# Three norm roots leave the inputs of products and go into their results; two products end tile by tile

## The reference

```python
def _rmsnorm(x, g):
    xf = x.astype(jnp.float32)
    y = xf * lax.rsqrt(jnp.mean(xf * xf, axis=-1, keepdims=True) + EPS)
    return (y * g.astype(jnp.float32)).astype(x.dtype)

        hn = _rmsnorm(x, norm_mix[l])
        z = hn @ w_in[l]
        ...
        x = x + _memory_cross_attention(_rmsnorm(x, norm_cross[l]), _rmsnorm(mem, norm_mem[l]),
                                        w_q_mem[l], w_kv_mem[l], w_o_mem[l])
        x = x + _peer(_rmsnorm(x, norm_ffn[l]), w_query[l], sub_keys[l], expert_u[l], expert_v[l])
```

## Time and profile before

| | us |
|---|---|
| median of 3 runs (lowest, highest) | 2040.69 (2038.19, 2043.49) |
| profiled execution, its own time | 2043.17 |
| its span, first to last instruction | 2041.3 |
| TensorE busy in it | 1978.3 |

### The profile page before, as it was taken

The page is one execution under the profiler, slowest core; times in us unless marked ns, Lnnn a source line. Parts: engine busy times, 40 slices in busy tenths (PEclk is TensorE's granted clock), DMA queues, the critical chain, the costliest instruction groups (busy, mean ns, idle before and its releaser), DMA issues.

```text
span 2041.3 us, 34876 instructions
## 1 busy us (share of the span) xinstructions
PE 1978.3 (97%) x14212; PEld 1831.8 (90%) x14212; DVE 1408.3 (69%) x2543; ACT 1140.7 (56%) x1919; POOL 303.1 (15%) x328
## 2 busy tenths in 40 slices
PE   8999999999999989998999989999999999999997
PEld 5798998999888889998988989999999998888886
DVE  6777765888777667547746458898996765555554
ACT  5865533556666455435654454456677754444444
POOL 0010010000000000000000000028867940000000
PEclk9999999999999999998999999999999999999999
DMA  9465787346444347665433444554444445555553
GB/s 355 159 213 186 245 282 233 115 153 220 153 147 145 114 118 228 189 185 181 156 114 133 134 154 161 184 179 151 156 142 158 145 148 189 188 186 186 188 189 118
DMA packets 97743, 356.25 MB, mean 175 GB/s; under 512 B 11104, under 2 KB 11232, under 8 KB 97200
## 3 DMA queue, kind: packets, MB, share of 16 engines
q1 hardware_dynamic: 84240, 305.04, 44.8%
q0 software_dynamic: 12624, 48.08, 7.3%
q10 hardware_dynamic: 720, 0.91, 0.1%
HBM read 352.94 MB, written 1.05 MB: 173 GB/s over the span
## 4 chain that ended last, share of the span: by engine, by line
PE 90%; DVE 5%; ACT 3%; issue 1%; DMA 1%; ACTq 0%; DVEq 0%
PE psum L576 23%; PE psum L577 23%; PE psum L578 23%; PE psum L569 18%; PE psum L583 2%; DVE wl L1993 1%; ACT wh L1368 1%; ACT work L1356 0%; DMA araw<-in_ada_w 0%; DMA con<-in_con 0%; DVE xc L1973 0%; DVE cross_sq L1973 0%; ACT na L1356 0%; DVE head_squares L1973 0%; ACT C L1356 0%
## 5 line engine op out<-in xcount | busy, mean ns | idle before, releaser
L1993 DVE TENSOR_TENSOR wl<-raw,wh 128x1024 fp32r<-128x1024 f32 (+1 forms) x566 | 687.7, 1218 | 436.7 <-ACT wh L1368 436.1
L1368 ACT ACTIVATE wh<-raw 128x1024 fp32r<-128x1024 f32 (+1 forms) x566 | 594.0, 1050 | 448.8 <-PE psum L578 410.9
L576 PE MATMUL psum<-peer_hh,wh 128*128 128x256 f32 x1152 | 330.7, 287 | 3.6 <-DVE peer_hl L1965 3.6
L577 PE MATMUL psum<-peer_hl,wh 128*128 128x256 f32 x1152 | 326.2, 283 | 0.0
L578 PE MATMUL psum<-peer_hh,wl 128*128 128x256 f32 x1152 | 326.1, 283 | 0.0
L576 PEld LDWEIGHTS psum<-peer_hh,wh 128*128 128x128 f32 x1152 | 219.5, 191 | 3.9 <-issue 3.9
L578 PEld LDWEIGHTS psum<-peer_hh,wl 128*128 128x128 f32 x1152 | 217.5, 189 | 0.0
L577 PEld LDWEIGHTS psum<-peer_hl,wh 128*128 128x128 f32 x1152 | 217.5, 189 | 0.0
L576 PE MATMUL psum<-wh,csh 128*128 128x512 f32 x512 | 202.9, 396 | 0.0
L578 PE MATMUL psum<-wh,csl 128*128 128x512 f32 x512 | 202.7, 396 | 0.0
L577 PE MATMUL psum<-wl,csh 128*128 128x512 f32 x512 | 202.7, 396 | 0.0
(11 more groups left out here) (456 smaller groups left out, 4675.8 us busy)
## 6 DMA issues: line engine op xcount, KB each, us to landing
raw<-in_mlp_w SPq DMA_DIRECT2D x128, 512.0 KB, 4.2
raw<-in_eu SPq DMA_DIRECT2D x128, 512.0 KB, 3.5
raw<-in_ev SPq DMA_DIRECT2D x128, 512.0 KB, 3.4
araw<-in_ada_w POOLq DMA_DIRECT2D x76, 512.0 KB, 4.8
raw<-in_dil_qk SPq DMA_DIRECT2D x48, 512.0 KB, 4.0
raw<-in_dil_v SPq DMA_DIRECT2D x24, 512.0 KB, 3.5
raw<-in_w_in SPq DMA_DIRECT2D x16, 512.0 KB, 3.6
raw<-in_w_query SPq DMA_DIRECT2D x16, 512.0 KB, 3.5
```

What stands on the lines that cost most here:

```text
L576: e.matmul(o, l[0], r[0], start=start, stop=False, skip_group_check=loose)
L577: e.matmul(o, l[0], r[1], start=False, stop=False, skip_group_check=loose)
L1368: e.activation(b.wh[v % NSPLIT][:, 0:cols], b.raw[v % NRAW][:, 0:cols], ACT.Copy).then_inc(S.hi, 1)
L1993: e.tensor_tensor(b.wl[v % NSPLIT][:, 0:cols], b.raw[v % NRAW][:, 0:cols], b.wh[v % NSPLIT][:, 0:cols].bitcast(F32), ALU.subtract).then_in ...
```

## The change

The second product of both MLPs gets another layout of its weights (`stationary`, regrouped on the host): four units hold all 32 input tiles of one output tile, so the output tiles end one after another, every four units, each in a bank of its own. Squares and sums are made tile by tile (`tile_square`, `tile_sum`); the sum of tile k is issued two units into the next tile. In the second MLP the tile is also multiplied by the next norm's gain and split at once (`tile_high`, `tile_low`), without the root.

For n4, n5 and n6 the root no longer stands in the product's input. It is made beside the first units of the next product (`root_x`, `rsqrt`) and multiplies results: in the mixer x_lru and gate by VectorE (`scaled`), q and k by GpSimd, v by ScalarE through a column per token; at n5 as a column in the softmax's scale; at n6 as a column in the experts' scores. `root_columns` turns the root's row into columns by two matmuls with one output column each. The experts' first product keeps an input with the root, made by VectorE, ScalarE and GpSimd beside query units 2 to 5. The last two units of w_o are done together, output pair by output pair (`rows_end`). `opening` is no longer used at these three borders. GpSimd scales mem, fills the bias masks and starts mem's load when the last MLP unit is done. The mixer's side work is placed anew. n2 keeps `norm_x`, with its sums made per tile.

```diff
-    beside = {3: ("conv", 0), 4: ("conv", 1), 5: ("conv", 2), 6: ("conv", 3), 8: ("gates", 0), 9: ("lam", 0),
-              10: ("decay", 0), 12: ("scan", 0)}
-    steps = {20: 0, 21: 1, 22: 2, 23: 3, 24: 4, 25: 5, 26: 6, 27: 7, 28: 8, 29: 9}
+    beside = {3: ("conv", 0), 4: ("conv", 1), 6: ("conv", 2), 8: ("conv", 3), 10: ("gates", 0), 11: ("lam", 0),
+              12: ("decay", 0), 14: ("scan", 0)}
+    steps = {19: 0, 21: 1, 22: 2, 23: 3, 24: 4, 25: 5, 26: 6, 27: 7, 28: 8, 29: 9}
...
-        if 1 <= i < 8:
+        if i in (1, 2, 3, 7, 9, 15, 16):
...
 def cross_order():
-    out = [("unit", "w_mem_v", 4), ("total", None, None)] + [("unit", "w_mem_v", i) for i in (5, 6, 7)]
+    out = [("unit", "w_mem_v", 4), ("tiles", None, 0), ("total", None, None), ("unit", "w_mem_v", 5),
+           ("tiles", None, 4), ("unit", "w_mem_v", 6), ("root", None, None), ("unit", "w_mem_v", 7)]
     for i in range(8):
         out.append(("unit", "w_q_mem_2", i))
+        if i == 0:
+            out.append(("columns", None, None))
         if i in (2, 4, 6):
             out.append(("step", None, i // 2 - 1))
...
     for c in range(16):
         out.append(("query", c, None))
+        if c == 0:
+            out += [("root", None, None)]
+        if c == 2:
+            out.append(("columns", None, None))
+        if c in (2, 3, 4, 5):
+            out += [("tile", 2 * c - 4, None), ("tile", 2 * c - 3, None)]
+        if c == 6:
+            out.append(("tile", 8, None))
...
+    def tile_sum(tag, k, ring):
+
+        if k == 0:
+            take(tag, "total")
+        ps = b.psum[:, at["bank", tag, "total"], :]
+        pe.wait_ge(S.act, at[tag, "square", k])
+        mm(ps[:, 0:256], ones, ring[:, (k % 4) * 256:(k % 4) * 256 + 256], k == 0, k == 7, mark=(tag, "squares", k),
+           loose=True)
+        if k == 7:
+            give(tag, "total", sem=S.act, key=(tag, "ms"))
+
+    def root_columns(tag, rs):
+
+        ps = take(tag, "roots")
+        pe.wait_ge(S.dve, at[tag, "root"])
+        for t in range(2):
+            mm(ps[:, t:t + 1], rs[:, t * 128:t * 128 + 128], ident[:, 0:1], True, True,
+               mark=(tag, "roots") if t else None)
+        give(tag, "roots", sem=S.dve, key=(tag, "root columns"))
...
+    def rows_end(tag, name, k, x, ring):
+
+        j = [weights(name, k), weights(name, k + 1)]
+        for c in range(8):
+            o = b.psum[:, at["bank", tag, c // 2], (c % 2) * 256:(c % 2) * 256 + 256]
+            for y in range(2):
+                w, done = wsp(j[y], c * 128, 128), y == 1 and c % 2 == 1
+                mm(o, w[0], x[y][0], False, False, loose=True)
+                mm(o, w[0], x[y][1], False, False, loose=True)
+                if c == 7:
+                    e.matmul(o, w[1], x[y][0], start=False, stop=done, skip_group_check=True).then_inc(S.unit, 1)
+                else:
+                    mm(o, w[1], x[y][0], False, done, loose=True, mark=(tag, "done", c // 2) if done else None)
+            if c in (5, 7):
+                square_sums(tag, c // 2 - 2, ring)
+        for c2 in range(4):
+            give(tag, c2, sem=S.dve, key=(tag, "out", c2))
 
...
         project((tag, 1), "mlp_w1", 4096, m.hh, lambda k: (S.dve, (norm, "lo", k)), S.act, first=32 * layer)
-        acc = [take(tag, 2, i) for i in range(4)]
-        for s in range(32):
-            j = weights("mlp_w2", 32 * layer + s)
-            pe.wait_ge(S.dve, at[(tag, 1), "h1", s // 2])
-            for c in range(8):
-                o, w, h = acc[c // 2][:, (c % 2) * 256:(c % 2) * 256 + 256], wsp(j, c * 128, 128), sp(m.h1, s)
-                if s == 31 and c in (1, 3, 5):
-                    mm(o, w[0], h[0], False, False, loose=True)
-                    mm(o, w[0], h[1], False, False, loose=True)
-                    mm(o, w[1], h[0], False, True, loose=True, mark=((tag, 2), "done", c // 2))
-                else:
-                    mm3(o, w, h, s == 0 and c % 2 == 0, s == 31 and c == 7, unit=c == 7, loose=True)
-        for c2 in range(4):
-            give(tag, 2, c2, sem=S.dve, key=((tag, 2), "out", c2))
-            square_sums((tag, 2), c2, m.rbf)
+        for c in range(8):
+            o = take(tag, 2, c)[:, 0:256]
+            for q in range(4):
+                j = weights("mlp_w2", 32 * layer + 4 * c + q)
+                for k in range(8):
+                    pe.wait_ge(S.dve, at[(tag, 1), "h1", 4 * q + k // 2])
+                    mm3(o, wsp(j, k * 128, 128), sp(m.h1, 8 * q + k), q == 0 and k == 0, q == 3 and k == 7,
+                        unit=k == 7)
+                if c and q == 1:
+                    tile_sum((tag, 2), c - 1, m.rbf)
+            give(tag, 2, c, sem=S.dve, key=((tag, 2), "out", c))
+        if layer == 0:
+            tile_sum((tag, 2), 7, m.rbf)
...
+    def tile_high(tag, ready, k, gain, dst):
+
+        ac.wait_ge(S.dve, at[ready])
+        act(dst[0][:, k * 256:k * 256 + 256], b.xs3[:, k, :], ACT.Copy, scale=gain, mark=(tag, "hi", k))
+
+    def root_x(tag, sums, tmp, last=3):
+        ac.wait_ge(S.pe, at[sums, "squares", last])
         act(tmp[:, 512:768], bank(sums, "total")[:, 0:256], ACT.Abs_reciprocal_sqrt, scale=1.0 / 1024, bias=eps,
             mark=(tag, "rs0"))
         act(tmp[:, 256:512], bank(sums, "total")[:, 0:256], ACT.Identity, scale=1.0 / 1024, bias=eps,
             mark=(sums, "ms"))
...
         for s in range(32):
             unit("mlp_w2", 32 * layer + s)
-        for c2 in range(4):
-            square((tag, 2), c2, m.rbf, ((tag, 2), "out", c2))
+            if s and s % 4 == 0:
+                after(s // 4 - 1)
+        after(7)
...
+        norm_x("n2", ("mlp0", 2), shift, m.hh, m.work[:, 0:2048], m.vtf[:, 0:768], last=7)
...
+                if (name, i) == ("w_in_2", 0):
+                    root_x("n4", ("mlp1", 2), m.tmp, 7)
...
         for kind, name, i in CROSS_ORDER:
-            if kind == "total":
-                norm_x("n5", "out2", None, m.hh, m.sq, m.tmp, UNIT_OF["w_mem_v", 5])
+            if kind == "tiles":
+                for k in range(i, i + 4):
+                    tile_high("n5", ("out2", "out", k // 2), k, vc(b, "cross", k), x.hh)
+            elif kind == "root":
+                root_x("n5", "out2", m.tmp)
+            elif kind in ("total", "columns"):
...
+            if c2 == 3:
+                unit("w_o_mem_2", 7)
+                ahead(UNIT_OF["w_query_2", 1] - AHEAD)
+            for k in (2 * c2, 2 * c2 + 1):
+                tile_high("n6 gain", ("mo", "out", c2), k, vc(b, "ffn", k), x.hh)
             square("mo", c2, m.ring, ("mo", "out", c2))
 
     def peer():
         m = b.peer
         phase("peer")
...
+    def tile_low(tag, k, gain, dst):
+
+        z = slice(k * 256, k * 256 + 256)
+        ve.wait_ge(S.act, at[tag, "hi", k])
+        stt(dst[1][:, z], b.xT[:, z], gain, dst[0][:, z].bitcast(F32), ALU.mult, ALU.subtract, mark=(tag, "lo", k))
...
+                if bias is None:
+                    tt(st[:, 1, i, :], st[:, 0, i, :], scale, ALU.mult, mark=(tag, "negmax", i))
+                else:
+                    ts(st[:, 1, i, :], st[:, 0, i, :], -scale, None, ALU.mult, mark=(tag, "negmax", i))
...
+        def after(c):
+
+            ve.wait_ge(S.unit, UNIT_OF["mlp_w2", 32 * layer + 4 * c + 3] + 1)
+            src = bank(tag, 2, c)[:, 0:256]
+            g, xs, mark = b.mod[:, 48 * layer + 40 + c:48 * layer + 41 + c], b.xs3[:, c, :], ((tag, 2), "out", c)
             if layer:
                 t = m.sq[:, c * 256:c * 256 + 256]
                 stt(t, src, g, xs, ALU.mult, ALU.add)
                 own()
                 cp(xs.rearrange("p (l s r) -> p l s r", l=16, s=4), t.rearrange("p (r s l) -> p l s r", r=4, s=4),
                    mark=mark)
+                own()
             else:
                 stt(xs, src, g, xs, ALU.mult, ALU.add, mark=mark)
+
+        mod_until(48 * layer + 40)
+        own()
+        for s in range(32):
+            c = s // 4 - 1
+            if c >= 0 and s % 4 == 0:
+                after(c)
+            unit("mlp_w2", 32 * layer + s)
+            if layer and c >= 0 and s % 4 == 0:
+                tile_low("n4", c, vc(b, "norm_mix_2", c), b.mix.hh)
+            tick(every)
+        after(7)
+        if layer:
+            tile_low("n4", 7, vc(b, "norm_mix_2", 7), b.mix.hh)
+        mod_until(last)
...
+
+        def scaled(c2, u):
+
+            c = 2 * (c2 % 2)
+            ve.wait_ge(S.unit, u + 1)
+            tt(m.ge[:, c:c + 2, :] if c2 > 1 else m.xp[:, c:c + 2, 3:259],
+               bank("in2", c2).rearrange("p (c t) -> p c t", c=2), rs.unsqueeze(1).broadcast_to([128, 2, 256]), ALU.mult,
+               mark=("in2", "out", c2))
...
+                if name == "w_in_2" and i % 2 and i < 8:
+                    scaled(i // 2, UNIT_OF[name, i])
...
-            if kind == "total":
-                norm_x("n5", lambda k: vc(b, "cross", k), None, m.hh, m.sq, m.tmp, UNIT_OF["w_mem_v", 5])
+            if kind == "tiles":
```

(51 more changed lines are left out.)

205 lines of the change are left out of this document (107 added, 98 removed).

## The result

| us | before | after |
|---|---|---|
| median (lowest, highest), 4 runs each | 2040.5 (2038.2, 2043.5) | 2019.1 (2017.2, 2019.3) |
| profiled execution | 2043.2 | 2019.0 |
| TensorE busy in it | 1978.3 | 1966.6 |

A forecast was written before the change was run, and what follows sets the result against it. TensorE, busy 97% of the span, bounds the kernel, so only its waits at stage borders count. Savings 9.8 + 0.3 + 6.5 + 5.3 - 0.7 = 21.2 us take the median from 2040.7 to 2019.5; likeliest range 2014 to 2025.

The forecast's parts named there:

- n4: Border from the second MLP's second product through the mixer's first five units: 29.0 us before, 19.2 after, 9.8 saved.
- n5: Border to the cross attention's query, through three query units: 15.6 us before, 9.0 after, 6.5 saved (bounds 4 and 7).
- n6: Border from w_o to the sixth expert query unit: 29.3 us before, 5.3 saved (bounds 3 and 7).
- the mixer: Mixer behind its first five units: lateness of 2.6 us against 2.9 before, 0.3 saved (bounds -4 and +2.9).
- n2: Border from MLP 0 to the dilated stage, its norm staying in place: 8.9 us before, 9.6 after, 0.7 lost.
- The seven interruptions at 0.1 each: In the MLP's second product, sums breaking the stream of units cost 0.1 us each (bounds 0 and 0.2).
- the stall at k = 7 of 0.2: First mixer unit: TensorE waits 0.2 us for the last input tile, ready 2.2 us after the last MLP matmul.
- rival 3: Second MLP products: tile-end work delays VectorE's weight splits; slower by 6 us if the chain is 7.5, time 2047; chance 0.05.
- my estimate by the skill's rule: Mixer: GpSimd contention stretches thirteen VectorE splits by 0.16 us each, 2.1 in all, so the stage loses 1.8; rejected.
- Rival 1: Mixer: GpSimd's scaling of mem (8.6 us a half) or mem's transfer is slow, costing 7.2 us: 2026.7; chance 0.15.
- Rival 2: Cross and expert query borders: waits move into the weight splits, about 5 us at one, 3 at the other: 2029.5; chance 0.10.
- the dip at even odds: Border to the expert query: the stall lowers the clock once, costing 1.7 us, counted as 0.8.

## Why the prediction was right, and where it was not

- **n4**: the terms that I listed make 19.0, not 19.2, a slip of 0.2 in the sum. Measured are 18.65 beyond the old product's length, up to the fifth unit's end (109.79 - 91.14). The seven interruptions at 0.1 each were nothing, and the stall at k = 7 of 0.2 too. The weight splits kept up with the tile ends: rival 3 (a chain of over 5.8) had no wait anywhere in the product.
- **The mixer**: the step that failed is the one that priced GpSimd's work at no cost to VectorE. I rejected the rule of the Trainium skill (GPSIMD Engine Reference, Key points) by the split's mean of 1.218 over a span in which GpSimd works for 303 us. That mean was the wrong row, twice over: 246 of those 303 us are one kind of work, the 128x128 tensor_scalar of the experts, and most of the rest is the issuing of DMAs; and of the 552 splits of 128x1024 only 72 ran beside that work at all, where they took 1.25 on average for 1.22 alone. The rows of the kind in question stood in the trace of before, at the very border I was reading. VectorE's and GpSimd's timelines of before:

```profile
938.25 0.88 DVE L1973 SCALAR_TENSOR_TENSOR mix_sq<-xT,vec,mix_tmp 128x256 f32<-128x256 f32 x2
939.21 0.42 DVE L1965 TENSOR_TENSOR mix_hl<-mix_sq,mix_hh 128x256 fp32r<-128x256 f32 x1
939.55 1.35 DVE L1973 SCALAR_TENSOR_TENSOR mix_sq<-xT,vec,mix_tmp 128x256 f32<-128x256 f32 x2
```

```profile
939.66 0.96 POOL L2808 TENSOR_TENSOR mix_hl<-mix_sq,mix_hh 128x256 fp32r<-128x256 f32 x1 [2.42 <-ACT mix_hh L1356]
```

  The same pair takes 0.88 alone and 1.35 beside it. The Trainium skill's finer rule (SBUF — State Buffer, Who interferes with whom) says that VectorE instructions with two SBUF inputs contend with GpSimd instructions that read SBUF and not with those that only write it, and that VectorE's copy and tensor_scalar can contend with any. The trace agrees on each: splits and scan stretched beside scaling and products, a split not beside a fill, a tensor_scalar beside a fill held to its end. A full block of the later one it states for VectorE's two-port modes, and the tensor_scalar held to the fill's end looks like it; the split, with two inputs, began 0.4 into a GpSimd scaling of 2.86 and was only 0.55 longer.
- The term was -3.5 instead of 0.3: 1.5 to 2.0 are the clock dip at 990.5 (4 of 8 traces with the wait of 1.8 have it), the rest is waits. Without the dip the stage loses 1.4 to 1.9 against before. That my estimate by the skill's rule, a loss of 1.8, lies there is in part luck: it took 0.16 for each of thirteen instructions, and measured are 0.2 to 0.9 for the ones that were hit.
- mem's scaling by GpSimd: 2.86 a half against 3.2 taken, and four times VectorE's 0.7. Rival 1 (8.6 a half) fell; that its transfer is late, also named in it, was half right: it landed at 5.9 for 5.4, and the slack was 0.2 (waits begin above 5.6) where I had 0.7.
- **n5**: 8.98 for three query units and their columns against 9.0; no wait. Rival 2 fell. The price of the eight low parts (3.22) was read from instructions with one input in PSUM; a low part takes 0.48, so 3.8. The room was large enough for that.
- **n6**: forecast a stall of 1.75, measured 1.2 and 0.3 ahead of a sum; the dip at even odds didn't come, and none of the twelve other traces has one there.
- **n2**: forecast a loss of 0.7, measured a gain of 1.2. Interruptions cost nothing (0.7); behind the product 5.6 against my 5.9; and the old product had taken 92.16 where the same one of MLP 1 took 91.14, which I hadn't looked at. The clock is 0.50 from 355.7 to 362.4 (6.8 us; so in ten of the thirteen traces with the change). That lies mostly behind this stretch, and it is no loss: before has two such dips of 3.4, at 358.4 and 368.7, and from the first dilated matmul to MLP 1's second product it takes 478.6, after 477.3.
- Of "what would show it": waits under 2.2 held (0 at n4, 0 at n5, 1.2 at n6), clock 1.00 at both starts held, sums without a wait held, five mixer units 15.6 after the last MLP unit against 16. "Waits above 3 in the mixer" for rival 1 didn't occur singly; five small ones did.

The total was right partly by luck, by cancelling: n2, n4 and n6 gave 3.5 more than forecast, and the mixer and the stretches between 4.4 less.

## What to carry to other kernels

Where a root or another factor per token stands between two products, apply it to the result: the next product then waits for no norm. Making the inputs tile by tile beside the last product is a second, smaller gain (here a fifth to a third). When work moves to GpSimd, price what it does to VectorE's instructions beside it, from a row of the same kinds of instruction on both engines, never from a mean over the kernel. A change that removes a wait at a border is paid for in the stretch behind it, where the moved work lands: walk that stretch instruction by instruction.

## What was not expected of the hardware

- A plain fp32 sum between fp32r matmuls shows 0.24 us and costs 0.43 to 0.45.
- The contention works in the other direction too: with two columns, two of GpSimd's products of q took 2.90 us together beside VectorE's product ia*xc and a split, of 1.22 each; two of k by the scan took 0.93. Each pair ends with a VectorE instruction (974.15 with the split's 974.10, 983.92 with the scan's 983.93), as if it had waited for that.
- The last product ran 0.5% faster in every trace of a changed kernel (357.59 us in all thirteen, 359.29 in the one trace of before), at the same granted clock. Its code is the same; the cause stays open.
